# Layer ends of a two-block transformer kernel: the last chunk read from PSUM, turns round four banks, conversions and sums reordered

## The reference

```python
h = rms_norm(x, g_pre_mix) * (1.0 + scale_m) + shift_m
z = h @ w_in                      # split: c_q, c_kv, k_rope, q_g, k_g, v_g, a_g, r_g
o = concat([mla_mixer(...), gla_mixer(...)]) @ w_out
x = x + gate_m * rms_norm(o, g_post_mix)
h = rms_norm(x, g_pre_ffn) * (1.0 + scale_f) + shift_f
f = (silu(h @ w_ffn_gate) * (h @ w_ffn_up)) @ w_ffn_down
x = x + gate_f * rms_norm(f, g_post_ffn)
```

## Time and profile before

| | |
|---|---|
| median of 3 runs | 2847.32 us (2845.05 to 2853.71) |
| the profiled execution's own time | 2843.03 us |
| its span, first to last instruction | 2841.3 us |
| TensorE busy | 2650.7 us (93%) |
| VectorE busy | 1660.7 us (58%) |
| ScalarE busy | 1158.0 us (41%) |
| mean granted clock of TensorE | 0.961 |

### The profile page before, as it was taken

How to read it: one execution, slowest core, us unless ns; L and a number is a source line. 1 busy time by engine, 2 the same in 40 slices (tenths; PEclk the granted TensorE clock), 3 DMA queues, 4 the chain that set the end, 5 groups by cost and what they waited for, 6 DMA issues and landing times.

```text
span 2841.3 us, 31125 instructions
## 1 busy us (share of the span) xinstructions
PE 2650.7 (93%) x12261; PEld 2197.7 (77%) x12261; DVE 1660.7 (58%) x1686; ACT 1158.0 (41%) x1211; POOL 0.2 (0%) x4
## 2 busy tenths in 40 slices
PE   5899978879999999998899999899789999999997
PEld 4678757768888888887788888778667888888886
DVE  7768657856665555556445666554555555555556
ACT  4234434433333333333435445434553333333333
POOL 0000000000000000000000000000000000000000
PEclk8899979999999999999899999999999999999999
DMA  8879747967776555654474445355345555555553
GB/s 312 311 267 316 284 160 252 323 138 250 251 250 221 183 189 191 192 187 159 132 225 147 148 141 166 131 181 192 110 142 178 192 183 189 189 192 192 187 186 129
DMA packets 267856, 566.01 MB, mean 199 GB/s; under 512 B 9807, under 2 KB 46573, under 8 KB 258686
## 3 DMA queue, kind: packets, MB, share of 16 engines
q1 hardware_dynamic: 265710, 561.73, 58.9%
q10 hardware_dynamic: 2064, 3.15, 1.0%
HBM read 559.60 MB, written 5.24 MB: 199 GB/s over the span
## 4 chain that ended last, share of the span: by engine, by line
PE 79%; DVE 9%; ACT 5%; issue 4%; DMA 2%; SPq 1%; DVEq 0%; ACTq 0%
PE bank L1160 24%; PE bank L1162 24%; PE bank L1161 24%; ACT wh L596 3%; DVE wl L1829 2%; DVE ACC L1999 2%; DVE ROWB L1829 1%; PE bank L1131 1%; DMA raw<-in_w_in 1%; PE bank L1234 1%; DVE X L1952 1%; PE bank L1695 1%; SPq L434 1%; PE bank L1196 1%; PE bank L1529 1%
## 5 line engine op out<-in xcount | busy, mean ns | idle before, releaser
L1829 DVE TENSOR_TENSOR wl<-raw,wh 128x2048 fp32r<-128x2048 f32 (+4 forms) x434 | 975.3, 2248 | 941.1 <-ACT wh L596 940.6
L596 ACT ACTIVATE wh<-raw 128x2048 fp32r<-128x2048 f32 (+4 forms) x434 | 816.3, 1881 | 1250.2 <-PE bank L1162 1137.2
L1160 PE MATMUL bank<-wh,XTh 128*128 128x512 f32 (+4 forms) x2680 | 1050.2, 392 | 45.0 <-DVE wl L1829 39.9
L1162 PE MATMUL bank<-wh,XTl 128*128 128x512 f32 (+4 forms) x2680 | 1037.1, 387 | 0.0
L1161 PE MATMUL bank<-wl,XTh 128*128 128x512 f32 (+4 forms) x2680 | 1036.4, 387 | 0.0
L1160 PEld LDWEIGHTS bank<-wh,XTh 128*128 128x128 f32 x2680 | 509.4, 190 | 148.9 <-issue 28.5
L1162 PEld LDWEIGHTS bank<-wh,XTl 128*128 128x128 f32 x2680 | 508.5, 190 | 95.8
L1161 PEld LDWEIGHTS bank<-wl,XTh 128*128 128x128 f32 x2680 | 509.9, 190 | 92.2 <-issue 0.2
L1160 PE MATMUL bank<-wh,HTh 128*128 128x512 f32 x704 | 277.3, 394 | 9.4 <-DVE HTl L1829 3.6
L1162 PE MATMUL bank<-wh,HTl 128*128 128x512 f32 x704 | 274.8, 390 | 0.0
L1161 PE MATMUL bank<-wl,HTh 128*128 128x512 f32 x704 | 274.8, 390 | 0.0
(11 more groups left out here) (296 smaller groups left out, 1437.2 us busy)
## 6 DMA issues: line engine op xcount, KB each, us to landing
raw<-in_w_ada SPq DMA_DIRECT2D x96, 1024.0 KB, 5.8
raw<-in_w_in SPq DMA_DIRECT2D x48, 1024.0 KB, 5.2
raw<-in_w_ffn_gate SPq DMA_DIRECT2D x44, 1024.0 KB, 5.2
raw<-in_w_ffn_up SPq DMA_DIRECT2D x44, 1024.0 KB, 5.2
raw<-in_w_ffn_down SPq DMA_DIRECT2D x44, 1024.0 KB, 5.0
raw<-in_w_gate SPq DMA_DIRECT2D x44, 1024.0 KB, 5.1
raw<-in_w_up SPq DMA_DIRECT2D x44, 1024.0 KB, 5.2
raw<-in_w_down SPq DMA_DIRECT2D x44, 1024.0 KB, 5.1
```

The source lines that it names most:

```text
L596: act.activation(wh[:, st.lin % 2, 0:width], raw[:, st.raw % 4, 0:width], ACT.Copy).then_inc(hi_made, 1)
L1160: pe.matmul(out_, hi_t[:, k, rows], w[0][:, q, :], start=first and q == 0, stop=False)
L1162: mm = pe.matmul(out_, lo_t[:, k, rows], w[0][:, q, :], start=False, stop=last and q == n - 1)
L1829: return dve.tensor_tensor(out_, a, b, op)
```

## The change

- All turns of eight groups are `WIDE`; `turn_into` turns groups 4 and 5 ahead of slab 0, and 6 and 7 ahead of slab 1.
- `last_squared` and `weigh_last` square and weigh the last chunk of `o`, `mix` and `xo` straight from its two banks, each engine on one bank at a time; `chunk_left` counts the chunk afterwards. `root_table` runs a square root of one column ahead of the layer's end in all five output layers.
- In the query layer `hi` of the next slab stands ahead of each evacuation.
- `mod_sum(3)` stands behind the attention loop.
- Between `o` and `f1` the additions go row block by row block; ScalarE squares 512 columns behind each; row 0 is normed whole and row 1 in four pieces, all on VectorE; each group of the turn waits for its piece only. `mod_fin(4)` stands behind the additions.
- The first four chunks of `w_in_2` are written out in place of a loop, and the turn of `z2` is woven with them; the square sums come behind the fourth conversion.
- In the last chunk of both feed-forwards `weigh(n-1)` stands ahead of `add(n)`.

```diff
-WIDE = {"mem", "x"}
+WIDE = {name for name, n, _ in TURNS if n == 8}
...
+            def root_table():
+                act.activation(rooted[:, :], eps[:, :], ACT.Sqrt)
...
             for c in range(3):
-                if c:
-                    hi()
-                    skip()
+                hi()
+                skip()
                 chunk_evac(CHUNK0["uq"] + c, lambda r: qrow[r][:, :, :].rearrange("p h d -> p (h d)")[:, 512 * c:512 * c + 512],
                            512, scale=QKD ** -0.5, done=45 + c)
-            hi()
-            skip()
...
+            def last_squared(name, layer, done):
+                m, c = 4 * RB * POST.index(name) + RB * 3, CHUNK0[layer] + 3
+                act.wait_ge(slab_used, done)
+                for r in range(RB):
+                    act.wait_ge(S("part_sq"), m + r - 3)
+                    if r:
+                        act.wait_ge(S("weighed"), m + 1)
+                    f(JUNK[:, 512 * ((m + r) % 4):512 * ((m + r) % 4) + 512], PB[2 * (c % 2) + r][:, :], ACT.Square,
+                      "part_sq", accum_out=psq[:, POST.index(name), r, 3:4])
+            def chunk_left(name):
+                act.wait_ge(S("weighed"), 4 * RB * (POST.index(name) + 1))
+                act.activation(rooted[:, :], eps[:, :], ACT.Copy).then_inc(chunk_out, RB)
...
-            chunk_squared("o", "wout", 3, st.lin - 1)
+            root_table()
+            last_squared("o", "wout", st.lin - 1)
             post_root("o")
+            chunk_left("o")
...
-                    norm_stats(pre, lambda r: X[:, r, :], D, after)
-                    norm_rows(pre, lambda r: X[:, r, :], lambda r: ROWB[:, r, :])
+                    j = NORMS.index(pre)
+                    for r in range(RB):
+                        for c in range(4):
+                            act.wait_ge(S("x_added"), 4 * r + c + 1)
+                            if c + r:
+                                act.wait_ge(S("x_sq"), 4 * r + c)
+                            f(JUNK[:, 512 * c:512 * c + 512], X[:, r, 512 * c:512 * c + 512], ACT.Square, "x_sq",
+                              accum_out=xsq[:, r, c:c + 1])
+                            if (r, c) in ((1, 0), (1, 3)):
+                                act.wait_ge(S("squared"), RB * j + r + (c == 3))
+                                part = slice(0, 1) if c == 0 else slice(1, 2)
+                                f(nstat[:, j, 1, part], nstat[:, j, 0, part], ACT.Sqrt, "row_rooted" if c == 0 else "rooted",
+                                  scale=1.0 / D, bias=eps[:, 0:1])
...
                 y_all = 8 * (FN + 1) * (k + 1)
+                root_table()
...
-            turn_hi("z2", XTh, gain=vT[:, V_LN_MIX:V_LN_MIX + KT])
-            norm_stats("z2", lambda r: X[:, r, :], D, "y1")
-            act.wait_ge(S("rooted_inv"), NORMS.index("z2") + 1)
...
+            turn_hi("z2", XTh, gain=vT[:, V_LN_MIX:V_LN_MIX + KT], between=lambda: hi(4 * width))
+            def z2_first(c):
+                chunk_evac(CHUNK0["zin2"] + c, lambda r: Z2[:, r, c * width:c * width + width], width, scale=z2_scale,
+                           done=st.lin - 2)
+            for c in range(4):
+                for s in range(4):
+                    if c or s == 3:
+                        hi(4 * width)
+                    if (c, s) == (0, 3):
+                        norm_stats("z2", lambda r: X[:, r, :], D, "y1")
+                    if (c, s) == (1, 0):
+                        act.wait_ge(S("rooted_inv"), NORMS.index("z2") + 1)
+                    if c and s == 0:
+                        z2_first(c - 1)
             hi(4 * width)
-            with act.Fori(0, 2) as i, st.loop(i, 2, 8, 8):
-                for c in range(2):
-                    for _ in range(4):
-                        hi(4 * width)
-                    act.wait_ge(slab_used, st.lins(-2))
-                    for r in range(RB):
-                        act.activation(Z2[:, r, bass.ds(i * (2 * width) + c * width, width)], PB[2 * (c % 2) + r][:, 0:width],
-                                       ACT.Copy, scale=z2_scale(r)).then_inc(chunk_out, 1)
+            z2_first(3)
...
+                    if name == "f1":
+                        pe.wait_ge(S("normed"), RB * 3 + 1 + b // 2 + 1)
+                    if name == "o" and b == 3:
+                        pe.wait_ge(S("mod_ready"), 10)
...
                     pe.wait_ge(S("turn_free"), TURN0[name] + 2 * s + 2)
-                    first_slab(s)
                     if s < 2:
                         turn(name, src, lambda: None, range(4 + 2 * s, 6 + 2 * s), after)
+                    first_slab(s)
...
-                if t == MH + 1:
-                    for _ in range(7):
-                        st.next(False)
-                    pe.wait_ge(S("masked"), MH)
-                    mod_sum(3)
...
+            for _ in range(7):
+                st.next(False)
+            pe.wait_ge(S("masked"), MH)
+            mod_sum(3)
...
-                                      lambda: None if k else pe.wait_ge(S("normed"), RB * 4),
+                                      lambda: None,
...
-            turn("z2", lambda r, k: X[:, r, P * k:P * k + P], lambda: None, after="y1")
-            turned_ready("z2")
-            with pe.Fori(0, 2) as i, st.loop(i, 2, 8, 8):
-                for c in range(2):
-                    chunk(c, ALL, Z2_PARTS[0][1], free=i * 4 + RB * (CHUNK0["zin2"] + c - 1))
+            for c in range(4):
+                chunk(CHUNK0["zin2"] + c, ALL, Z2_PARTS[0][1], turning=None if c else (
+                    "z2", lambda r, k: X[:, r, P * k:P * k + P], lambda: None, "y1"))
...
+            def weigh_last(name, layer, done):
+                m, c = 4 * RB * POST.index(name) + RB * 3, CHUNK0[layer] + 3
+                dve.wait_ge(slab_used, done)
+                for r in (1, 0):
+                    if r == 0:
+                        dve.wait_ge(S("part_sq"), m + 1)
+                    tt(ROWB[:, r, 1536:D], PB[2 * (c % 2) + r][:, :], G[:, 1536:D], ALU.mult).then_inc(S("weighed"), 1)
+            def add_normed(name, weighed=False):
                 j, q = NORMS.index(name), POST.index(name)
                 dve.wait_ge(S("part_sq"), 4 * RB * (q + 1))
                 dve.tensor_reduce(nstat[:, j, 0, :], psq[:, q, :, :], AX.X, ALU.add).then_inc(S("squared"), RB)
-                weigh(name, 3)
+                if not weighed:
+                    weigh(name, 3)
...
+                if name == "o":
+                    return
                 for c in range(4):
                     for r in range(RB):
-                        x, y = (t[:, r, 512 * c:512 * c + 512] for t in (X, ROWB))
-                        dve.scalar_tensor_tensor(x, y, nstat[:, j, 2, r:r + 1], x, ALU.mult, ALU.add).then_inc(S("x_added"), 1)
+                        x_add(j, r, c)
+            def x_add(j, r, c):
+                x, y = (t[:, r, 512 * c:512 * c + 512] for t in (X, ROWB))
+                dve.scalar_tensor_tensor(x, y, nstat[:, j, 2, r:r + 1], x, ALU.mult, ALU.add).then_inc(S("x_added"), 1)
...
+            weigh_last("o", "wout", st.lin - 1)
+            add_normed("o", True)
+            j, n = NORMS.index("o"), NORMS.index("f1")
+            for c in range(4):
+                x_add(j, 0, c)
+            x_add(j, 1, 0)
+            dve.wait_ge(S("x_sq"), 4)
+            dve.tensor_reduce(nstat[:, n, 0, 0:1], xsq[:, 0, :], AX.X, ALU.add).then_inc(S("squared"), 1)
+            x_add(j, 1, 1)
+            x_add(j, 1, 2)
+            x_add(j, 1, 3)
+            dve.wait_ge(S("row_rooted"), 1)
+            dve.reciprocal(nstat[:, n, 2, 0:1], nstat[:, n, 1, 0:1]).then_inc(S("row_inv"), 1)
             mod_fin(4)
-            add_normed("o")
+            dve.wait_ge(S("row_inv"), 1)
+            dve.wait_ge(S("x_added"), 4 * RB)
+            dve.tensor_scalar(ROWB[:, 0, :], X[:, 0, :], nstat[:, n, 2, 0:1], None, ALU.mult).then_inc(S("normed"), 1)
+            dve.wait_ge(S("x_sq"), 4 * RB)
+            dve.tensor_reduce(nstat[:, n, 0, 1:2], xsq[:, 1, :], AX.X, ALU.add).then_inc(S("squared"), 1)
+            dve.wait_ge(S("rooted"), n + 1)
+            dve.reciprocal(nstat[:, n, 2, 1:2], nstat[:, n, 1, 1:2]).then_inc(S("rooted_inv"), 1)
+            dve.wait_ge(S("rooted_inv"), n + 1)
+            for c in range(4):
+                cols = slice(512 * c, 512 * c + 512)
+                dve.tensor_scalar(ROWB[:, 1, cols], X[:, 1, cols], nstat[:, n, 2, 1:2], None, ALU.mult).then_inc(S("normed"), 1)
             def ffn(k, pre, gain, shift, more):
-                if k == 0:
-                    norm_row2(pre)
...
-                    add(n, FN - 1, last)
-                    if n == 0 and k:
+                    if n == 1 and k:
                         dve.wait_ge(S("gain_in"), 48)
                     if n:
                         weigh(("y1", "y2")[k], n - 1)
+                    add(n, FN - 1, last)
...
-            turn_lo("z2", XTh, XTl, gain=vT[:, V_LN_MIX:V_LN_MIX + KT])
```

(24 more changed lines are left out.)

4 lines of the change are left out of this document (2 added, 2 removed).

## The result

The changed kernel takes 2796.97 us, the median of 4 executions (2791.3 to 2797.41), against 2848.07 of the kernel before (2845.05 to 2853.71, 4 executions): 0.9816 of it, 95% interval 0.9801 to 0.9832. The forecast was 2809.7, with 2796 to 2826 as range. It had the sign, and it had the gain at the layer ends where it is.

What follows compares the result with a forecast made beforehand. TensorE, busy 93% of the span, was taken as the bound, so gains lay only in its waits at layer seams. Terms summed to -37.6 us, giving 2809.7 from the 2847.3 median, range 2796 to 2826.

Steps and rivals of the forecast that it cites:

- query and key slabs: Query and key stage: converting the next slab's high part before the evacuation shortens TensorE's waits of 5.39; -13.5 us (-11 to -15.6).
- Rival 1: Query and key stage: VectorE or the loads take the gain back; total about -24, 2823 us; chance 0.12.
- the weighing: Ends of both feed-forwards: `weigh(n-1)` ahead of `add(n)` lengthens the slab cycle; +3.65 us at the first, +1.0 net at the second.
- Rival 2: Feed-forward ends: the weighing costs nothing because the squares do not gate the conversion; -4.65 more, about 2805 us; chance 0.10.
- rival 4: Seams: something else holds the banks and slab 0 waits as before; about -15 (2832 us) or nothing; chance 0.05.
- with durations of the same instructions in this execution: All seams: each edit costed as the shift of TensorE's next slab, using instruction durations from the one profiled execution.
- sum and turn of `o`: Behind attention: moving `mod_sum(3)` hides the heads' normalising, and four banks save a stop; -2.7 us (-1.5 to -4.5).
- My -14.2: `o` to first feed-forward: no evacuation, early table load, row-wise additions, norm in pieces, four banks; -14.2 us (-8 to -16.5).
- `z2`: First feed-forward's end: woven turn starts slabs earlier; -3.1 us net of the weighing's loss (+1 to -6.8).
- The rows show the next instruction right behind the load: Seams: reason for costing a hoisted table load at 1.28 us, not the Trainium skill's about 2.66 with the drain.
- Rival 3: Five seams: transpositions ahead of slab 0 keep TensorE's clock low through four slabs each; 72 us lost, 2882 us; chance 0.05.
- `xo` to `f2`: `xo` to second feed-forward: slightly later start, but the norm ahead of VectorE's memsets begins 3 earlier; -2.8 us (-1.5 to -4).

## Why the prediction was right and wrong

- **Right: what bounds it, and where.** All of the gain is at the seams; the stretches within layers moved by 0 to 0.8. One sign of the forecast could tell nothing: clocks under 0.7 at the seams were to speak against it, and the transpositions ahead of slab 0 stand at 0.50 in both kernels.
- **Right: query and key slabs**, -12.5 to -13.1 against -13.5, alone and in the whole. Rival 1 fell.
- **Right: the weighing.** +3.4 and +1.0 against +3.65 and +1.0. The edit that spoke against itself was a loss, and undoing it gives 4.4 in the stretches. Rival 2 fell, and rival 4 too: the banks did free slab 0.
- **Wrong: "with durations of the same instructions in this execution".** This is the step that failed. It mis-sized two terms. `mod_sum(3)` was held at 6.82 and takes 3.72; its move was priced at 2.0 and is worth 2.9 to 3.9, and with the banks (next point) sum and turn of `o` gave 6.7 where 2.7 was said. And at `f1` slabs 0 and 1 of before were held at 6.68 and 5.73, which in three of five traces with two banks are 7.5 to 7.6 and 8.3. My -14.2 is near the first pair of traces (105.8 to 91.3 is -14.5), but that is luck: the trace I costed from was one with the fast slab 1. The mean is -17.9. Over four traces of the old seam and nine of the new it is 109.0 against 90.5.
- **Wrong: the price of the four banks.** In my sum they had 1.0 at `o`, 6.2 at `f1` and nothing named elsewhere, by a later split some 4.5: 12 in all. Alone they give 25.7, in the changed kernel 18, and at `o` 3.0 to 3.6. At `f1` they take out two pairs of waits and the level loss behind them; at `xq` and `f2` they turn a stop of 2.73 inside the turn into one of 1.8 to 2.2.
- **Mis-sized: `z2`**, -5.5 against -3.1: banks and weaving together give 8.9, not 6.75, and I credited the weaving with all of it.
- **Misread: the row behind the load.** "The rows show the next instruction right behind the load" is not so at the seam of the earlier trace rows, where the root waited 0.70 more for VectorE. Taken out again, the five hoists are worth some 2.7, and the price of 1.28 for a load itself is right.
- **Rival 3 looked at the right thing with the wrong sign.** I let the level only cost. At `f1` with four banks it was up by the end of slab 0 in every trace, in spite of the transpositions ahead; with two it was low in slab 1 in three of five. The Trainium skill (TensorE: Matmul & The Clock Gate, What's actually happening) says, of a kernel's start, that the moment of the change differs from run to run of the same kernel. Here it differs in mid-kernel too: the two traces of before are 5.5 apart at one seam, and this was the reason not to price from one.
- **Not right either: the -1.4 at `xo` to `f2`** (said -2.8). Three kernels with a longer chain there have 74.1 to 74.7, below the changed kernel's 77.1, with 97.6 to 98.2 ahead of it. Together the two seams take two values, about 172 and 175. They differ in the level: where `xq` is 97.7 and not 94.8, its slab 0 takes 7.3 and not 5.7, and the first eight matmuls of the cross attention, behind a wait of 0.74, take 3.7 and not 2.0. What picks the level stays open.

With the measured sizes (-12.8, -6.7, -17.9, -5.5, -6.9, +0.8) the terms reach -49.0, and the medians show 49 to 51. That is bookkeeping and no second proof: the sizes are stretches of the same traces.

## What to carry to other kernels

Price a seam from two or three traces of the same kernel: where the same matmuls behind the same wait differ by half, the mean is the base, and a change that removes the wait also removes that loss. A pause between two slabs cost itself and, in three of five traces, 2.6 us of the slab behind it, so take the pauses out (more banks, work in one run) before shortening the chain ahead of them. Where two edits act on the same seam, measure each with and without the other before giving either its share. Filling a wait with idle matmuls gave nothing that the time could show, since another engine's chain decided when the wait ended.

## What the runs showed of the hardware

The 32 matmuls of `mod_sum(3)`, one column each, run without a gap. At the old place they follow a wait of 2.78 and three transpositions. There they stood at 1.2 GHz from end to end in four traces (6.82 to 6.83 us), and all but the first two in a fifth (6.65). Windows over them and over what follows, in the kernel before:

```profile
444.50:451.30 6.80, 6.80 (x34) 6.80 (x33) 0.00 (x0) 2.29 (x2) 0.00 (x0) 0.50 0.22 92
451.30:454.50 3.20, 2.77 (x13) 2.48 (x12) 1.13 (x5) 0.00 (x0) 0.00 (x0) 0.50 0.00 0
```

At the new place twelve products of 128 columns stand between them and the wait, at 1.2 GHz for 2.6 us. The level then rose at the sum's start or within its first five matmuls, and it was low again within 0.6 us of the sum's end in every such trace. Windows over the products, the sum and the turn, in the changed kernel:

```profile
427.30:429.90 2.60, 2.60 (x15) 2.60 (x14) 0.78 (x3) 2.29 (x2) 0.00 (x0) 0.50 0.49 202
429.90:433.60 3.70, 3.70 (x34) 3.70 (x34) 0.78 (x3) 0.00 (x0) 0.00 (x0) 0.96 0.00 0
433.60:436.70 3.10, 3.10 (x16) 3.10 (x16) 3.05 (x4) 1.59 (x3) 0.00 (x0) 0.50 0.00 0
```
